# A hybrid decoder layer with 32 experts: blocks in the order of their numbers, earlier weight loads, five seams rearranged

## The chip, the cores and the metric

The kernel runs on one core of one Trainium2 chip. The metric is the device time of one execution in microseconds. Before the change three runs took 1807.75 to 1808.81 us, with a median of 1807.97 us. The engines are TensorE (PE), VectorE (DVE), ScalarE (ACT), GpSimd (POOL) and SyncE (SP, which here only issues DMAs).

## The reference

One layer on x of 1024 tokens by 1024 features, in float32:

```
h = rms_norm(x, g);  proj = h @ w_in          # q, k, v of four mixers, and 4 x 1024 gate columns
o_swa = sliding-window attention (128 back, sinks, T5 bias)
o_fox = forgetting attention;  o_sb = stick-breaking attention
o_dsa = attention on the 256 best keys of an indexer, T5 bias
merged = sum over the 4 branches b of sigmoid(gate_b) * (o_b @ w_branch[b])
x = x + merged @ w_out
h2 = rms_norm(x, g2)
# 32 experts in 4 groups: best group, its 2 best experts, weights from both softmaxes
# assignments sorted by expert, each expert's padded to blocks of 128 tokens; block i, of expert e:
  g, u = split(h2[tokens of i] @ w_up[e], 2);  y = (silu(g) * u) @ w_down[e]
x = x + weighted sum of each token's two y
```

An expert's `w_up` is 1024 x 1024 and its `w_down` 512 x 1024, 6 MB in all.

## The kernel before

**Products.** Operands are kept as two parts that TensorE takes, a high one that ScalarE writes by rounding and a low one that VectorE or GpSimd writes as the difference. Each product is three matmuls: high by high, and high by low both ways.

**Stages.** `build` runs stages one after the other. Between two of them all engines meet at a barrier.

- `project` norms and turns the eight x tiles (SyncE's first issues, then `turn_x` on TensorE), makes V tile by tile, then 17 pieces of q and k columns and the indexer's scores. ScalarE's high parts and GpSimd's low parts of the weight pieces run ahead of TensorE.
- `select_and_gate` multiplies 32 pieces of gate columns, each 48 matmuls of 128x512 (`sg_gp`, lines 83 to 85), ScalarE takes the sigmoid and the tile is stored. Behind piece 0 TensorE makes the small T5 products of line 893, for which two tables are loaded. VectorE picks the best 256 keys all through this stage.
- `mix` does the attention head by head, then merges the branches: for each of 8 column blocks k and 4 branches j, 12 matmuls into `at_sps` (two banks by turns), which VectorE multiplies by a gate tile in `selm` and adds up (lines 1506, 1511, 1515). VectorE also makes the low part of the next branch weights (`wb_lo`, line 1463, after j = 2) and at some blocks that of an output weight (`wo_lo`, after j = 1). The output projection, the norm and the router follow tile by tile; SyncE stores x2 and h2 of each tile.
- `route_and_experts` counts the experts' tokens, places them (VectorE, a list of small steps), and runs the blocks.

**The experts.** Each block needs four pairs of up weights and two of down weights, 1 MB each. They pass through `WeightRing`: 12 raw places that SyncE loads (`load_pair`, line 1762), then 4 places with the parts (`split_high`, line 1766, ScalarE; `split_low`, line 1770, VectorE). SyncE waits for the low part of what lay in a place before. An expert's number comes from a plan (`eblk`). Before the plan is made, SyncE can load only expert 0's pairs, in the routing stage. All blocks of an expert follow one another, and experts are taken in the order 0, 8, 16, 24, 1, 9, ... (`spread`, `stride`).

GpSimd gathers the tokens of blocks 0 and 1 (line 2139) by numbers that VectorE finds (`find_next`, `number_tokens`) with sums by TensorE (`sum_ids`), and writes 16 notes, one for each tile of tokens and choice, into `slots` (line 2144). Later blocks read their token ids from `slots`, so these must have landed. Two empty scatters to the output open the row of scatters (line 2134), which go one after another since a token can be in two blocks. The loop then runs two blocks a trip. A block is `turn_x`, `up` (48 matmuls into `ex_gp`, `ex_upp`), `turn_a`, and `down` (24 matmuls into `ex_yp`); ScalarE's `silu` and `scale` (line 2247) stand between. The block after has its `up` ahead of this block's `down`. The last two blocks are written out behind the loop.

## Time and profile before

| what | value |
| --- | --- |
| median of 3 runs | 1807.97 us |
| the profiled execution's own time | 1811.79 us |
| its span in the profile | 1810.1 us |
| TensorE busy | 1695.0 us, 94% |
| VectorE, ScalarE, GpSimd busy | 1268.5 (70%), 859.0 (47%), 348.6 (19%) |
| DMA | 361.72 MB, mean 200 GB/s |
| ScalarE's high part of an expert pair (L1766), mean of 192 | 1915 ns |
| VectorE's low part of one (L1770), mean of 192 | 2288 ns |
| landing of an up pair, a down pair, median | 20.7, 21.2 us |
| mean granted clock of TensorE | 0.976 |

The page cuts the span in 40 slices of 45 us. In most of them TensorE is busy nine tenths or more:

```profile
PE   6999998999999988899998999677999999999995
DVE  4023678799999508877657753486898989888883
GB/s 198 90 109 170 79 136 116 133 118 93 93 94 93 130 91 170 82 106 140 144 13 228 225 128 125 202 326 317 383 370 374 352 362 346 363 346 365 366 361 55
```

The projection takes slices 1 to 7, the gates 8 to 15, attention 16 to 21, merging, output projection and router 22 to 25, the routing 26 and 27, and the experts the rest. A digit is the busy share of a slice in tenths, 9 for 90% or more. Busy time of an engine that nobody waits for costs nothing, so what counts is who waits for whom at a given moment; the timeline gives that, with the idle time ahead of an instruction and what released it in brackets.

### The profile page before, as it was taken

Reading aid. Unit: us, or ns where it says so; the run is one execution under the profiler, and the core shown is the slowest. Engines: PE = TensorE matmul, PEld = TensorE weight load, DVE = VectorE, ACT = ScalarE, POOL = GpSimd, SP = SyncE. Lnnn points to the kernel's source line nnn. Section 1 sums busy time; section 2 is a strip of 40 time slices with the busy share of each in tenths; the row PEclk is TensorE's granted clock in tenths of the full one; section 3 lists DMA queues with packets and bytes.
Section 4 is the critical chain, followed back from the end, with each engine's and each line's share of the span. In section 5 each row is a group of like instructions: output and inputs, shape, how many; then the busy total and the mean of one; then the engine's idle time right before and its main releaser. Section 6 shows DMA issues by size and latency. Waiting matters only on the chain. (4 is left out here: it accounts for less than half of the span.)

```text
span 1810.1 us, 25235 instructions
## 1 busy us (share of the span) xinstructions
PE 1695.0 (94%) x8628; PEld 1405.5 (78%) x8628; DVE 1268.5 (70%) x1693; ACT 859.0 (47%) x1034; POOL 348.6 (19%) x289
## 2 busy tenths in 40 slices
PE   6999998999999988899998999677999999999995
PEld 5887777787888877799986778566888888877784
DVE  4023678799999508877657753486898989888883
ACT  6114552211112215567851112345888887777773
POOL 3111122232222210100010000173222222222221
PEclk9999999999999998999999999878999999999997
DMA  5236233332222437346506634588999999999992
GB/s 198 90 109 170 79 136 116 133 118 93 93 94 93 130 91 170 82 106 140 144 13 228 225 128 125 202 326 317 383 370 374 352 362 346 363 346 365 366 361 55
DMA packets 110578, 361.72 MB, mean 200 GB/s; under 512 B 18731, under 2 KB 22827, under 8 KB 110496
## 3 DMA queue, kind: packets, MB, share of 16 engines
q1 hardware_dynamic: 97508, 342.52, 54.4%
q0 software_dynamic: 12992, 18.14, 4.2%
q8 instruction: 51, 0.84, 0.2%
q14 instruction: 27, 0.22, 0.0%
HBM read 315.51 MB, written 63.96 MB: 210 GB/s over the span
## 5 line engine op out<-in xcount | busy, mean ns | idle before, releaser
L1770 DVE TENSOR_TENSOR ex_wl<-ex_raw,ex_wh 128x2048 fp32r<-128x2048 f32 x192 | 436.5, 2288 | 92.1 <-ACT ex_wh L1766 89.1
L1766 ACT ACTIVATE ex_wh<-ex_raw 128x2048 fp32r<-128x2048 f32 x192 | 367.3, 1915 | 110.6 <-DMA ex_raw<-in_w_expert_up 53.3
L83 PE MATMUL sg_gp<-hT_hi,gs_wh 128*128 128x512 f32 x512 | 200.8, 392 | 6.7 <-PEq L66 6.7
L84 PE MATMUL sg_gp<-hT_lo,gs_wh 128*128 128x512 f32 x512 | 200.2, 391 | 0.0
L85 PE MATMUL sg_gp<-hT_hi,gs_wl 128*128 128x512 f32 x512 | 200.0, 391 | 0.0
L793 ACT ACTIVATE gs_wh<-gs_raw 128x1024 fp32r<-128x1024 f32 x30 | 31.8, 1061 | 263.9 <-PE sg_gp L85 263.9
L857 DVE MATCH_REPLACE8 selm<-sg_top,selm 128x512 f32<-128x512 f32 (+5 forms) x160 | 138.6, 872 | 0.0
L853 DVE MAX8 sg_top<-selm 128x8 f32<-128x512 f32 (+5 forms) x160 | 133.9, 876 | 0.0
L2335 PE MATMUL ex_gp<-ex_wh,ex_xh 128*128 128x512 f32 x256 | 109.0, 426 | 17.6 <-DVE ex_wl L1770 14.6
L1627 PE MATMUL at_ops<-at_v,at_pT 128*128 128x65 f32 (+1 forms) x984 | 125.0, 269 | 0.0
L1627 PEld LDWEIGHTS at_ops<-at_v,at_pT 128*128 128x128 f32 x984 | 120.5, 192 | 0.7
L737 POOL TENSOR_TENSOR gs_wl<-gs_raw,gs_wh 128x1024 fp32r<-128x1024 f32 x30 | 72.2, 2405 | 251.2 <-ACT gs_wh L793 251.2
L83 PEld LDWEIGHTS sg_gp<-hT_hi,gs_wh 128*128 128x128 f32 x512 | 96.7, 189 | 28.1 <-issue 8.0
L84 PEld LDWEIGHTS sg_gp<-hT_lo,gs_wh 128*128 128x128 f32 x512 | 96.7, 189 | 20.4 <-issue 0.2
L85 PEld LDWEIGHTS sg_gp<-hT_hi,gs_wl 128*128 128x128 f32 x512 | 96.7, 189 | 20.2
L590 PE MATMUL pj_ps<-hT_hi,gs_wh 128*128 128x512 f32 x272 | 110.5, 406 | 0.0
L2335 PE MATMUL ex_yp<-ex_wh,ex_ah 128*128 128x512 f32 x256 | 102.2, 399 | 7.8 <-DVE ex_al L2046 7.8
L591 PE MATMUL pj_ps<-hT_lo,gs_wh 128*128 128x512 f32 x272 | 106.1, 390 | 0.0
L592 PE MATMUL pj_ps<-hT_hi,gs_wl 128*128 128x512 f32 x272 | 106.1, 390 | 0.0
L2134 POOL DMA_INDIRECT out_x<-ex_xa,ex_ids_o x32 | 57.4, 1794 | 235.7 <-ACT ex_xa L2247 235.4
L2335 PE MATMUL ex_upp<-ex_wh,ex_xh 128*128 128x512 f32 x256 | 102.0, 398 | 0.0
L2337 PE MATMUL ex_gp<-ex_wh,ex_xl 128*128 128x512 f32 x256 | 101.8, 398 | 0.0
(311 smaller groups left out, 3672.3 us busy)
## 6 DMA issues: line engine op xcount, KB each, us to landing
ex_raw<-in_w_expert_up SPq DMA_DIRECT2D x128, 1024.0 KB, 20.7
ex_raw<-in_w_expert_down SPq DMA_DIRECT2D x64, 1024.0 KB, 21.2
gs_raw<-in_w_gate SPq DMA_DIRECT2D x32, 512.0 KB, 3.5
gatesT<-sg_go SPq DMA_DIRECT2D x32, 512.0 KB, 2.6
selm<-gatesT SPq DMA_DIRECT2D x32, 512.0 KB, 5.9
at_qk<-qkh SPq DMA_DIRECT2D x52, 256.0 KB
at_qk<-qkl SPq DMA_DIRECT2D x44, 256.0 KB
gs_raw<-in_w_qk SPq DMA_DIRECT2D x17, 512.0 KB, 4.9
```

Source lines behind the costliest of these rows:

```text
L83: pe.matmul(out, a_hi, b_hi, start=(k == 0), stop=False)
L84: pe.matmul(out, a_hi, b_lo, start=False, stop=False)
L85: last = pe.matmul(out, a_lo, b_hi, start=False, stop=(k == len(lhs) - 1))
L590: pe.matmul(out, wh[k % 2][:, q, :], hT[0][:, q, cols], start=(q == 0), stop=False)
L591: pe.matmul(out, wh[k % 2][:, q, :], hT[1][:, q, cols], start=False, stop=False)
L592: last = pe.matmul(out, wl[k % 2][:, q, :], hT[0][:, q, cols], start=False, stop=(q == KC - 1))
L853: dve.max(top8[j][:, :], acc).then_inc(picked, 1)
L857: dve.match_replace(acc, top8[j][:, :], acc, PICKED).then_inc(picked, 1)
L1627: last = pe.matmul(o_ps[u % 2][:, 0:width], pT[u % 2][:, j, :], values[:, kb, f:f + width], start=(j == 0), stop=(j == len(ks) - 1))
L1766: act.activation(ring.wh[r][:, :, :], ring.raw[slot][:, :, :], ACT.Copy).then_inc(ring.w_high, 1)
L1770: dve.tensor_tensor(ring.wl[r][:, :, :], ring.raw[slot][:, :, :], ring.wh[r][:, :, :].bitcast(F32), ALU.subtract).then_inc(ring.w_low, 1)
L2335: pe.matmul(bank, hi[:, k, :], wh[r][:, i, cols], start=(k == 0), stop=False)
```

## The change

1. **Start.** The gain vector is issued second and x tile 1 fourth; TensorE turns two tiles before the first V tile, not three.
2. **Projection to gates.** The banks of both stages are the same now, and `project` multiplies gate piece 0 at its end.
3. **Gates to attention.** GpSimd writes the two one-column memsets of `keep` before the four large ones.
4. **Merging.** `wb_lo` goes after j = 1 and `wo_lo` after j = 2.
5. **Early loads.** The ring's raw places have a fixed address from the start, in an order in which four of them are free in `mix`: expert 0's up pairs are loaded behind tiles 1 to 4 of h2.
6. **Order of the experts.** Block e, for e under 32, is the first block of expert e; further blocks of an expert follow from block 32 on. So expert 1's up pairs are loaded without the plan. VectorE has four steps more, two on 128x256 numbers and two on small ones.
7. **Routing.** `sum_ids(2)` comes after the first up pair, ScalarE makes three high parts before the last exponential, and TensorE runs 11 matmuls whose result nobody uses (`keep_busy`) around the first `turn_x`.
8. **End.** The last block's down weights are split earlier, its turned activations go to block x's buffers (`xh`, `xl`), its matmuls go to `ex_gp` and `ex_upp`, and `turn_a` of the last block stands between the two down pairs of the one before. The last scaling is done in two halves.

The diff, cut to its core:

```diff
@@ -275,9 +277,9 @@
                     sp.dma_start(o[k], t[:, :].bitcast(F32)).then_inc(stored, 16)
             load_x(0)
+            sp.dma_start(g[:, :], a["norm_mix_g"].to_broadcast([P, D])).then_inc(g_loaded, 16)
+            load(0)
             load_x(1)
-            load(0)
-            sp.dma_start(g[:, :], a["norm_mix_g"].to_broadcast([P, D])).then_inc(g_loaded, 16)
             load_x(2)
...
-            for t in range(3):
-                turn_x(t)
-            turns = [{1: 3, 5: 4}, {1: 5, 5: 6}, {1: 7}]
+            turn_x(0)
+            turn_x(1)
+            turns = [{1: 2, 5: 3}, {1: 4, 5: 5}, {1: 6, 5: 7}]
...
+            pe.wait_ge(w_low, GATE_PIECE + 1)
+            pe.wait_ge(rectified, len(UNITS))
+            side = GATE_PIECE % 2
+            for h in range(2):
+                cols = slice(h * HALF, (h + 1) * HALF)
+                multiply(pe, si[:, cols], [(wh[side][:, q, :], wl[side][:, q, :]) for q in range(KC)],
+                         [(hT[0][:, q, cols], hT[1][:, q, cols]) for q in range(KC)])
...
+            pe.sem_inc(gated, 2)
             for k in range(NG):
                 pe.wait_ge(w_low, GATE_PIECE + k + 1)
                 for h in range(2):
+                    if k == 0:
+                        continue
...
+                if 1 <= tile <= len(IN_ROUTE):
+                    load_pair(sp, a, ring, IN_ROUTE[tile - 1], 0, tile - 1)
...
+            for s in range(2):
+                pool.memset(keep[s][:, T:T + 1], 1.0).then_inc(made, 1)
+            pool.wait_ge(made, 2)
             slots.zero(pool, (2, 3))
             pool.wait_ge(slots.zeroed, 8)
-            for s in range(2):
-                pool.memset(keep[s][:, T:T + 1], 1.0).then_inc(made, 1)
...
-                if j == 2 and 2 <= k + 1 < KC:
+                if j == 1 and 2 <= k + 1 < KC:
                     wb_lo(k + 1)
-                if j == 1 and k in (2, 4, 6):
+                if j == 2 and k in (2, 4, 6):
                     wo_lo(k // 2)
...
@@ -1884,22 +1911,19 @@
         position = lambda b, j: (b + 1) * PAIRS + j
         place = lambda s, j: ((s + 1) % 2 * PAIRS + j) % RAW
         SKIPPED = UP_PAIRS
-        CONSTS = 14
+        CONSTS = 16
         marks = {}
         @block.sync
         def _(sp):
-            for j in IN_ROUTE:
-                load_pair(sp, a, ring, j, 0, j - FIRST)
             for j in range(UP_PAIRS, PAIRS):
                 load_pair(sp, a, ring, PAIRS + j, 0, j)
+            for j in range(UP_PAIRS):
+                load_pair(sp, a, ring, place(0, j), 1, j)
             sp.wait_ge(planned, 1)
             sp.wait_ge(gathered[0], 16)
             n = trips(sp)
             expert = lambda b: sp.value_load(eblk[0:1, bass.ds(b, 1)], min_val=0, max_val=EXPERTS - 1)
-            e = expert(1)
-            for j in range(UP_PAIRS):
-                load_pair(sp, a, ring, place(0, j), e, j)
...
+            step(dve.scalar_tensor_tensor(base[:, :], base[:, :], float(P), to_end[:, :], ALU.mult, ALU.add))
             dve.wait_ge(ranked, 1)
-            step(dve.scalar_tensor_tensor(slot, base[:, :].unsqueeze(1).to_broadcast([P, NT, EXPERTS]), float(P), ranks,
-                                          ALU.mult, ALU.add))
+            E = [P, NT, EXPERTS]
+            step(dve.scalar_tensor_tensor(slot, ranks, P - 0.5, base[:, :].unsqueeze(1).to_broadcast(E), ALU.is_ge, ALU.mult))
+            step(dve.tensor_tensor(slot, slot, ranks, ALU.add))
+            step(dve.tensor_tensor(slot, slot, first[:, :].unsqueeze(1).to_broadcast(E), ALU.add))
...
+            step(dve.tensor_tensor(ebcol[:, :], ebcol[:, :], own[:, :], ALU.add))
...
+            find_next(3)
             x_lo(1, 1)
-            find_next(3)
-            number_tokens(3)
             low(0, 0, 0)
             gate_up(0, position(0, 0))
+            number_tokens(3)
...
+            low(n * 2 + 1, 1, UP_PAIRS, SKIPPED)
             gate_up(n * 2 + 1, position(n * 2, UP_PAIRS))
-            for j in range(UP_PAIRS, PAIRS):
-                low(n * 2 + 1, 1, j, SKIPPED)
-            a_lo(n * 2 + 1)
+            low(n * 2 + 1, 1, UP_PAIRS + 1, SKIPPED)
+            a_lo(n * 2 + 1, xh[0], xl[0])
...
-            const(pool.memset(steps[:, 0:1], -1.0))
-            const(pool.memset(stride[:, :].rearrange("p (j q) -> p j q", q=GROUPS)[:, 0:PER_GROUP - 1, GROUPS - 1],
-                              1.0 - PER_GROUP * (GROUPS - 1)))
+            const(pool.memset(steps[:, 0:1], 4.0 * T))
+            const(pool.affine_select(out=own[:, :], in_=own[:, :], compare_op=ALU.is_ge, fill=0.0, base=EXPERTS - 1,
+                                     pattern=[[0, 1]], channel_multiplier=-1))
+            const(pool.iota(first[:, :], pattern=[[P, EXPERTS]], base=0, channel_multiplier=0, **F))
+            const(pool.iota(to_end[:, :], pattern=[[-P, EXPERTS]], base=(EXPERTS - 1) * P, channel_multiplier=0, **F))
...
-            const(pool.iota(bcol[:, :], pattern=[[0, 1]], base=0, channel_multiplier=1, **F))
-            const(pool.iota(evens[:, :], pattern=[[2, MAX_BLOCKS // 2]], base=0, channel_multiplier=0, **F))
+            const(pool.iota(bcol[:, :], pattern=[[0, 1]], base=-EXPERTS, channel_multiplier=1, **F))
+            const(pool.iota(evens[:, :], pattern=[[2, MAX_BLOCKS // 2]], base=-EXPERTS, channel_multiplier=0, **F))
...
-            high_in_route(IN_ROUTE[0])
+            for p in IN_ROUTE[:3]:
+                high_in_route(p)
             act.wait_ge(d, marks["ratio"])
             act.activation(rinv[:, :, :], ratio[:, :, :], ACT.Exp).then_inc(e_done, 1)
-            for p in IN_ROUTE[1:]:
-                high_in_route(p)
+            high_in_route(IN_ROUTE[3])
...
+            def last_high(j):
+                act.wait_ge(w_loaded[place(1, j)], loads(n, 1))
+                act.wait_ge(used, position(n * 2, j - 1))
+                split_high(act, ring, place(1, j), place(1, j) % RING)
+            last_high(UP_PAIRS)
             silu(n * 2 + 1)
+            last_high(UP_PAIRS + 1)
+            a_hi(n * 2 + 1, xh[0])
             scale(n * 2, 0, n, position(n * 2, PAIRS))
-            for j in range(UP_PAIRS, PAIRS):
-                act.wait_ge(w_loaded[place(1, j)], loads(n, 1))
-                act.wait_ge(used, position(n * 2, j))
-                split_high(act, ring, place(1, j), place(1, j) % RING)
-            a_hi(n * 2 + 1)
-            scale(n * 2 + 1, 1, n, position(n * 2 + 1, PAIRS) - SKIPPED)
+            act.wait_ge(ids_o_loaded[1], n * 16 + 16)
+            act.wait_ge(scattered[1], n * 16 + 16)
+            for h, bank in enumerate((gp, upp)):
+                act.wait_ge(last_made, h + 1)
+                last = act.activation(xa[1][:, h * HALF:(h + 1) * HALF], bank[:, :], ACT.Copy,
+                                      scale=ids_o[1][:, 1:2].bitcast(F32))
+            last.then_inc(scaled, 1)
...
+                if j == 0:
+                    sum_ids(2)
                 if j == 1:
                     turn_x(1, 1, 16)
-                    sum_ids(2)
+            def keep_busy(n):
+                for _ in range(n):
+                    pe.matmul(gp[:, :], ones[:, :], full[:, :, :, :].rearrange("p k t e -> p (k t e)"), start=True, stop=True)
...
+            keep_busy(6)
             turn_x(0, 0, 16)
+            keep_busy(5)
             up(0, 0, FIRST, FIRST, between)
...
-            down(n * 2, 0)
-            turn_a(n * 2 + 1)
-            down(n * 2 + 1, 1, SKIPPED)
+            down(n * 2, 0, lambda j: turn_a(n * 2 + 1) if j == UP_PAIRS else None)
+            pe.wait_ge(a_low, n * 2 + 2)
+            pe.wait_ge(w_low, position(n * 2 + 1, UP_PAIRS) + 1 - SKIPPED)
+            for h, bank in enumerate((gp[:, :], upp[:, :])):
+                cols = slice(h * HALF, (h + 1) * HALF)
+                for k in range(FC):
+                    if (h, k) == (0, PAIR):
+                        pe.wait_ge(w_low, position(n * 2 + 1, UP_PAIRS + 1) + 1 - SKIPPED)
+                    r = place(1, UP_PAIRS + k // PAIR) % RING
+                    pe.matmul(bank, xh[0][:, k, :], wh[r][:, k % PAIR, cols], start=(k == 0), stop=False)
+                    pe.matmul(bank, xh[0][:, k, :], wl[r][:, k % PAIR, cols], start=False, stop=False)
+                    last = pe.matmul(bank, xl[0][:, k, :], wh[r][:, k % PAIR, cols], start=False, stop=(k == FC - 1))
+                last.then_inc(last_made, 1)
```

VectorE's list in the merging of branches, from block k = 2 to k = 3, before (`mg_sum` and `at_v`/`at_o` are gated products and sums, `mg_wb_low` and `or_wo_low` the two low parts):

```order
L1506 TENSOR_TENSOR mg_sum<-at_sps,selm 128x1024
L1511 TENSOR_TENSOR at_v<-at_sps,selm 128x1024
L1515 TENSOR_TENSOR mg_sum<-mg_sum,at_v 128x1024
L1463 TENSOR_TENSOR or_wo_low<-or_wo_raw,or_wo_high 128x1024
L1511 TENSOR_TENSOR at_o<-at_sps,selm 128x1024
L1515 TENSOR_TENSOR mg_sum<-mg_sum,at_o 128x1024
L1463 TENSOR_TENSOR mg_wb_low<-mg_wb_raw,mg_wb_high 128x1024
L1511 TENSOR_TENSOR at_v<-at_sps,selm 128x1024
L1515 TENSOR_TENSOR mg_sum<-mg_sum,at_v 128x1024
```

The same place of the change:

```order
L1522 TENSOR_TENSOR mg_sum<-at_sps,selm 128x1024
L1527 TENSOR_TENSOR at_v<-at_sps,selm 128x1024
L1531 TENSOR_TENSOR mg_sum<-mg_sum,at_v 128x1024
L1479 TENSOR_TENSOR mg_wb_low<-mg_wb_raw,mg_wb_high 128x1024
L1527 TENSOR_TENSOR at_o<-at_sps,selm 128x1024
L1531 TENSOR_TENSOR mg_sum<-mg_sum,at_o 128x1024
L1479 TENSOR_TENSOR or_wo_low<-or_wo_raw,or_wo_high 128x1024
L1527 TENSOR_TENSOR at_v<-at_sps,selm 128x1024
L1531 TENSOR_TENSOR mg_sum<-mg_sum,at_v 128x1024
```

The branch weights' low part now stands two operations earlier, ahead of the third branch.

ScalarE's list behind the loop, before (`ex_gl` is the SiLU, `ex_xa` the scaled result, `ex_ah` the high part of the turned activations):

```order
L2235 ACTIVATE ex_gl<-ex_gp 128x512
L2246 REGISTER_ALU
L2247 ACTIVATE ex_xa<-ex_yp,ex_ids_o 128x1024
L2277 REGISTER_ALU
L2278 REGISTER_ALU
L1766 ACTIVATE ex_wh<-ex_raw 128x2048
L2278 REGISTER_ALU
L1766 ACTIVATE ex_wh<-ex_raw 128x2048
L2239 ACTIVATE ex_ah<-ex_ap 128x512
L2246 ISA
L2247 ACTIVATE ex_xa<-ex_yp,ex_ids_o 128x1024
```

The same place of the change:

```order
L1789 ACTIVATE ex_wh<-ex_raw_53 128x2048
L2265 REGISTER_ALU
L2266 ACTIVATE ex_gl<-ex_gp 128x512
L2307 REGISTER_ALU
L1789 ACTIVATE ex_wh<-ex_raw_54 128x2048
L2270 ACTIVATE ex_xh<-ex_ap 128x512
L2277 REGISTER_ALU
L2278 ACTIVATE ex_xa<-ex_yp,ex_ids_o 128x1024
L2319 ACTIVATE ex_xa<-ex_gp,ex_ids_o 128x512
L2319 ACTIVATE ex_xa<-ex_upp,ex_ids_o 128x512
```

Both high parts now stand ahead of the scaling of the block before, the first one ahead of the SiLU.

## Rows read from the trace of the kernel before

**Rows 1.** Expert loop: stretch, length, busy PE PEld DVE ACT POOL, PEclk, DMA share, GB/s.

```profile
1260.00:1440.00 180.00, 180.00 (x854) 149.04 (x853) 159.99 (x92) 145.25 (x101) 40.33 (x40) 1.00 1.01 371
1470.00:1700.00 230.00, 225.08 (x1051) 183.53 (x1051) 195.03 (x111) 176.36 (x124) 55.80 (x51) 1.00 0.99 358
```

**Rows 2.** Timeline, start: start, duration, engine, line, operation, [idle before, its releaser].

```profile
9.16 4.01 DVE L447 SCALAR_TENSOR_TENSOR pj_x<-pj_x,pj_rs,pj_g 128x1024 f32<-128x1024 f32 x2 [9.16 <-DMA pj_g<-in_norm_mix_g]
...
24.38 2.55 POOL L336 TENSOR_TENSOR pj_vl<-gs_raw,pj_vh 128x1024 fp32r<-128x1024 f32 x1 [0.83 <-ACT pj_vh L362]
```

**Rows 3.** Timeline, border from projection to gates, TensorE and VectorE.

```profile
318.27 0.77 PE L83 MATMUL sg_gp<-hT_hi,gs_wh 128*128 128x512 f32 x1 [6.68 <-PEq L66]
...
323.76 1.21 DVE L816 TENSOR_TENSOR sg_fg<-sg_fhl 4x1024 f32<-4x1024 f32 x1 [4.23 <-DMA sg_fbias<-in_forget_bias]
...
331.70 1.45 PE L893 MATMUL sg_tp<-sg_onehot,sg_table 33*4 33x384 f32 x4
```

**Rows 4.** Busy time by stretches, within the gates' stage.

```profile
450.00:600.00 150.00, 150.00 (x663) 124.20 (x662) 149.97 (x275) 28.35 (x42) 32.08 (x14) 1.00 0.27 95
```

**Rows 5.** Timeline, border from gates to attention.

```profile
682.74 0.42 DVE L1417 TENSOR_TENSOR_SCAN at_keep<-at_t 128x128 f32<-128x128 f32 x1 [68.12 <-POOL at_keep L1281]
...
683.54 0.48 PE L1602 MATMUL at_tps<-ident,at_x 128*128 128x128 f32 x1 [2.00 <-DVE at_x L1421]
```

**Rows 6.** TensorE's waits from 960 to 1045: total us, count, longest.

```profile
PE at_sps L83 <- DVE mg_wb_low L1463: 8.1, 6, 1.8
```

**Rows 7.** Timeline, merging: first and last of six waits, a gate tile.

```profile
967.28 0.50 PE L83 MATMUL at_sps<-o_hi,mg_wb_high 128*128 128x512 f32 x1 [0.97 <-DVE mg_wb_low L1463]
...
978.77 0.33 SPq L1208 DMA_DIRECT2D mg_wb_raw<-in_w_br  x1
...
983.63 1.22 DVE L1506 TENSOR_TENSOR mg_sum<-at_sps,selm 128x1024 f32<-128x1024 f32 x1 [0.86 <-DMA selm<-gatesT]
...
1031.70 0.50 PE L83 MATMUL at_sps<-o_hi,mg_wb_high 128*128 128x512 f32 x1 [1.70 <-DVE mg_wb_low L1463]
```

**Rows 8.** Waits of SyncE's queue, 1150 to 1250: total us, count, longest.

```profile
SPq L1762 <- DVE ex_wl L1770: 41.5, 12, 16.9
```

**Rows 9.** Timeline, routing and the first blocks of the experts.

```profile
1168.89 0.42 DVE L1980 SCALAR_TENSOR_TENSOR ex_xa<-rt_base,ex_yp 128x256 f32<-128x256 f32 x1
...
1195.38 1.05 POOL L2139 DMA_INDIRECT ex_xg<-h2d,rt_found  x1 [5.09 <-DVE rt_found L1995]
...
1238.98 1.11 ACT L2247 ACTIVATE ex_xa<-ex_yp,ex_ids_o 128x1024 f32<-128x1024 f32 x1 [14.62 <-DMA out_x<-ex_xa,ex_ids_o]
...
1244.27 0.80 PE L2335 MATMUL ex_gp<-ex_wh,ex_xh 128*128 128x512 f32 x1 [9.55 <-DVE ex_wl L1770]
```

**Rows 10.** Chain that ended last, 1155 to 1262: start, us, what.

```profile
1222.33 7.81 DMA slots<-rt_entry,rt_pos
...
1231.89 6.92 DMA out_x<-ex_xa,ex_ids_o
```

**Rows 11.** Timeline, TensorE behind a short idle, between the first two blocks.

```profile
1203.46 0.77 PE L2362 MATMUL ex_ap<-ident,ex_act 128*128 128x128 f32 x4 [3.19 <-DVE ex_act L2042]
...
1205.36 0.63 PE L2336 MATMUL ex_gp<-ex_wl,ex_xh 128*128 128x512 f32 x1
```

**Rows 12.** Timeline, the end.

```profile
1783.22 4.49 DVE L1770 TENSOR_TENSOR ex_wl<-ex_raw,ex_wh 128x2048 fp32r<-128x2048 f32 x2 [6.36 <-ACT ex_wh L1766]
...
1788.45 0.79 PE L2335 MATMUL ex_yp<-ex_wh,ex_ah 128*128 128x512 f32 x1 [7.77 <-DVE ex_al L2046]
...
1798.99 1.59 POOL L2134 DMA_INDIRECT out_x<-ex_xa,ex_ids_o  x1 [15.10 <-ACT ex_xa L2247]
```

**Rows 13.** One tile's issues and landings: last two down pairs, then the last scatter.

```profile
L1762 SPq DMA_DIRECT2D ex_raw<-in_w_expert_down x2: 1851/1937/2023, 1756.4 to 1758.6; - x2
...
DMA to landing us min/median/max: 19.0/19.7/20.5
...
DMA to landing us min/median/max: 6.4/6.4/6.4
```

More of the change, by code:

```diff
@@ L144, in __init__ @@
         self.out_parts = [sb(f"gs_out{part}", [P, T], FR) for part in ("_hi", "_lo")]
+        self.banks = [c.enter_context(nc.psum_tensor(f"gs_banks{s}", [P, KC, P], F32)) for s in range(2)]
         self.w_loaded = [sem(f"gs_w_loaded{s}") for s in range(3)]
@@ L2350, in up, with down @@
                         between(j)
-            def down(b, s, skipped=0):
+            def down(b, s, between=None):
                 pe.wait_ge(a_low, b + 1)
```

66 lines of the change are left out of this document (40 added, 26 removed).

## The prediction

> **What bounds the kernel now.** I read the page first: TensorE is busy 94% of the span. Such a share says little alone, so the next view is the busy time by stretches. Between 1260 and 1440 us TensorE is never idle while the DMA engines are full (share 1.01); from 1470 to 1700 they are still full and TensorE idles 4.9 us [rows 1]. So the experts run on two resources that are nearly equal, and giving one of them room can't bring much there. Most of the 115 us of TensorE idle lie elsewhere, in waits at the borders of stages. I then read the timeline at each border that the diff touches. The reader should see in each who releases TensorE, and who is next in line just behind: that decides how much of a wait is to be had. A result within 0.2% (3.6 us) is what a measurement of this kernel can't tell from no change.
>
> **Start.** VectorE waits until 9.16 for the gain vector, issued behind two x tiles and a weight piece [rows 2]. The change issues it second, and TensorE begins the first V tile after two turned tiles instead of three. But TensorE's way through that tile ends with GpSimd's low part of weight piece 3, at 24.38 + 2.55 = 26.93 [rows 2]. That part follows ScalarE's serial list (roots and high parts), full from 14 us on. In the new issue order x tile 1 comes last of the four, so I take this list as about 2 us earlier and piece 3 as 1.7 earlier. The tile turned later costs its eight transposes then, 0.7. **Gain 1.0**; ends 0 (x tile 1 as late as the gain vector is now, ScalarE unmoved) and 2.5.
>
> **From projection to gates.** TensorE idles 6.68 before 318.27 [rows 3]. The change puts gate piece 0 (48 matmuls at 150 / 663 = 0.226 [rows 4], 10.9 us) ahead of the barrier. The hole is shorter than the work: TensorE ends at 311.6 + 10.9 = 322.5, and with 1.3 for the barrier the next stage starts at 323.8, 5.5 later than now. There a wait comes out that was hidden. The small matmuls (331.70, 1.45) need the one-hot and T5 tables, which SyncE issues in the new stage behind the forget bias; VectorE got that bias at 323.76, 5.5 after the stage began [rows 3]. Until now 13 us of gate matmuls covered this. Now TensorE stands to about 323.8 + 6.1 = 329.9, and starts at half clock: small matmuls to 332.3, piece 1 10.9, plus 1.1 for its matmuls at half clock, so 344.3 against 331.70 + 1.4 + 10.9 = 344.0. **Loss 0.3**: a stall moved, not removed. Ends: loss 2, gain 1.5 (tables 2 us sooner). By the Trainium skill, DMA: Bandwidth & Descriptors, "Anatomy of one DMA", a transfer has a fixed cost of about 2 us; by that rule the tables are there some 4 us into the stage, and the part gains about 1.7. The 5.5 us of the row speak against it.
>
> **From gates to attention.** VectorE's first scan waits for two tiny memsets of GpSimd, which stand behind four large ones: it starts at 682.74, and TensorE, idle 2.00, at 683.54 [rows 5]. Put first, they are done before the first sigmoid is. What is late next is V, loaded in this stage: TensorE's first product with it would come 2 us sooner, and V maybe 1. The large memsets end 0.4 later; the loads behind them serve head 2, some 40 us on. **Gain 1.5**; ends 0.9 and 2.0.
>
> **Merging the branches.** Six times TensorE waits at a block's first product for the low part of the next branch weights, 8.1 us in all [rows 6]. The five blocks from 967.28 to 1031.70 take 12.88 each [rows 7]; their 48 matmuls take 10.9. The change makes that low part one branch earlier and the output weight's one later, as the order excerpt shows, and this wait ends. Late next is the gate tile: SyncE issues it only when the previous block's products are done (issues begin 978.77), and VectorE starts on it at 983.63, 4.9 later [rows 7]. The gated product ends 1.22 after, 6.1 after the block's start; TensorE's third product reuses that bank and could start at 5.5. So 0.6 or more of each wait comes back, and 0.3 in blocks where VectorE also carries the output weight (nine operations of about 1.2: 10.7 of 10.9). 12.88 becomes 11.8 to 11.9: five blocks give 5.0, the first 0.4. **Gain 5.4**; ends 3 and 8.1.
>
> **Routing, and the start of the experts.** Four early loads of 1 MB and expert 1's first four fill the ring sooner. Does this lead help later? SyncE waits 41.5 us for freed places before 1250, 16.9 of it at once [rows 8]: the ring of 12 is full already when the loop gets going. **So the early loads are worth nothing by themselves**; the lead that counts is the ring's size. What holds the loop is another chain: GpSimd's gather at 1195.38, then twelve notes and a gather, the last note landing 7.81 after 1222.33, the ids, two empty scatters landing 6.92 after issue; ScalarE scales at 1238.98 and TensorE, idle 9.55, starts at 1244.27 [rows 9, 10]. Three things move it. The added VectorE steps (two like the one at 1168.89, of 0.42 and a gap, two of some 0.2) delay it by 1.35. The gather of block 2 needs its token numbers, which the new order sums after one pair instead of two, with TensorE at full clock; GpSimd idles 5.09 there [rows 9]. VectorE's list after its routing steps (three low parts of 2.2, the low part of x, a search of 2.7, one more low part) ends at 1193.2, so the gather starts at 1194.2, 1.1 earlier. Last, with the weights ahead, 4 MB less are queued while notes and ids land. With nothing queued the last scatter landed in 6.4 [rows 13]; I take 2.3 off the three landings together. **Gain 3.4**; ends: loss 1 (only the added steps), gain 6.5 (every landing as with nothing queued).
>
> **End.** Now the last block's down weights are split only after the block before is scaled: VectorE's two low parts start at 1783.22, behind ScalarE's two; TensorE idles 7.77 before its last 24 matmuls, and the last scatter starts at 1798.99 [rows 12]. The new end splits these weights earlier and sums into free banks. But their loads are issued at 1756.4 and 1758.6 and land 19.0 and 20.5 later, 1775.4 and 1779.1 [rows 13]. ScalarE's list has the first split ahead of the SiLU: split (1.9, the mean of its 192) to 1777.4, SiLU 1778.0; VectorE's low part (2.2) to 1779.7, the product 1780.4. TensorE is done with the first down pair at 1777.4 (down ends at 1780.1 now, a pair is 2.7) and stands 3 us for the transposes. After 3.19 us of idle it ran at half clock (0.63 a row, starts 0.43 apart) [rows 11], so I take that again: second pair to 1786.1, block 30's scatter, some 2 us after, at 1788.2. It must land (6.5) before the last one starts: about 1795.0. The last products are done near 1791.8 and scaled by 1793.3; they no longer end last. **Gain 4.0**; ends 2, and 7.6 (clock kept: 1784.7 + 6.5).
>
> **Sum.** 1.0 - 0.3 + 1.5 + 5.4 + 3.4 + 4.0 = 15.0 us. The profiled execution took 1811.8; it becomes 1796.8. The median of the three runs lies 3.8 below that execution, so I forecast **1793 us**.
>
> **Rivals.** (A) The lead does count: 4.2 MB at 371 GB/s [rows 1] are 11 us of DMA work done early, and the 6 us that TensorE idles for weights late in the loop vanish: 15.0 + 6 gives 1787. For it: the DMA engines are the late bound. Against it: rows 8. Chance 0.10. (B) Covers hold everywhere: merging 8.1 and the end 7.6 give 6.3 more, 1787; with the tables early 1785. Against it: the second waiter in rows 7 and 13. Chance 0.15. (C) Covers fail: start 0, gates -2, merging 3, routing 0.5, the end 2, attention 1.5, so a gain of 5 and 1803. For it: each seam has a second waiter within 1 to 2 us. Chance 0.16. (D) Slower: in the order of numbers experts read neighbouring weights, where now the order strides over eight. If that costs DMA rate, it does so from 1244 to 1764, at 358 to 371 GB/s now [rows 1]. To lose the 15.0 in 520 us the mean rate must fall by 3%, under about 350; at 4% it is 20.8 longer, 1814. No row shows it; against it, each load is 1 MB in either order. Chance 0.03. (E) The change reorders the program but frees no wait that ends last: within 3.6 us, 1808. Chance 0.03.
>
> **Numbers.** The forecast, 1789 to 1797, has 0.53. The range 1784 to 1800 takes in A, most of B and the near part of C, and leaves out the rest. Faster by over 0.2%: 0.53 + 0.10 + 0.15 + 0.16 = 0.94; no change 0.03; slower 0.03.
>
> **What would show it.** Right: TensorE idle some 6 us inside the gates' stage before the small matmuls; no wait for the branch weights' low part, but short ones for a gated bank; the ring full before the loop, with ScalarE's first scale some 3 us earlier in the routing; TensorE idle about 3 us between the last two down pairs, and the last scatter waiting for the one before. Wrong: no idle at the small matmuls; no TensorE idle late in the loop (A); a DMA rate under 350 GB/s there (D); merging blocks still at 12.9 us, or at 10.9 (B).

## The result, and the profile after

Seven runs of the changed kernel took 1792.7 to 1805.9 us, with a median of 1801.6; seven of the kernel before 1807.4 to 1811.4, median 1808.5. The ratio is 0.9944, with a 95% interval of 0.9928 to 0.9960: 10.1 us faster, or 7 to 13. The two medians by themselves lie 6.9 apart, at the lower end of that interval. The forecast was 15, with 8 to 24 as its range. In these runs the changed kernel scatters over 13 us where the one before scatters over 4; the traces of the experiments point at a cause.

The page of the changed kernel, with the profiled execution at 1804.9 us:

```profile
span 1803.3 us, 25241 instructions
...
PE 1706.3 (95%) x8639; PEld 1405.0 (78%) x8639; DVE 1269.5 (70%) x1697; ACT 860.2 (48%) x1035; POOL 350.7 (19%) x292
...
PE   7999999899999998899999999688999999999995
...
PEclk9999999899999998999999999889999999999998
...
GB/s 194 97 112 171 80 130 117 134 118 93 94 94 93 124 98 170 83 106 132 153 13 210 246 152 176 190 298 299 376 369 372 358 363 352 351 356 353 366 354 76
```

TensorE is busy 11 us **longer** than before, at the same number of real products. That is the first thing to notice: something made its work slower. To find where the time went I took the same event in both traces at each border, and subtracted. Both profiled executions lie 3.3 us above the medians of their kernels, so the gains add up to 6.8, and each is read from one pair of traces.

| event (first of its kind) | before | after | gained so far | in this part | forecast |
| --- | --- | --- | --- | --- | --- |
| q and k products | 91.76 | 90.19 | 1.6 | 1.6 | 1.0 |
| attention, first scores | 679.07 | 677.75 | 1.3 | -0.3 | -0.3 |
| merging, first product | 941.49 | 939.95 | 1.5 | 0.2 | 1.5 |
| output projection | 1045.12 | 1042.84 | 2.3 | 0.7 | 5.4 |
| routing, first count | 1166.27 | 1165.48 | 0.8 | -1.5 | 0 |
| first up product | 1184.69 | 1185.20 | -0.5 | -1.3 | |
| turn_x of block 4 | 1260.40 | 1254.15 | 6.2 | 6.8 | 3.4 with the line above |
| turn_x of block 31 | 1751.28 | 1746.51 | 4.8 | -1.5 | 0 |
| end of the span | 1810.1 | 1803.3 | 6.8 | 2.0 | 4.0 |

The rows of the timeline of the changed kernel that answer to [rows 3], [rows 5] and [rows 7]:

```profile
326.88 2.71 PE L905 MATMUL sg_tp<-sg_onehot,sg_table 33*4 33x384 f32 x4 [5.99 <-DMA sg_table<-in_t_table]
...
679.24 0.42 DVE L1433 TENSOR_TENSOR_SCAN at_keep<-at_t 128x128 f32<-128x128 f32 x1 [65.95 <-ACT at_t L1310]
...
682.97 0.69 PE L1643 MATMUL at_ops<-at_v,at_pT 128*128 128x64 f32 x2 [0.96 <-DMA at_v<-vtok]
...
972.83 0.80 PE L83 MATMUL at_sps<-o_hi,mg_wb_high 128*128 128x512 f32 x1 [2.26 <-DVE mg_sum L1522]
...
1044.75 0.63 PE L1686 MATMUL at_tps<-or_wo_low,at_qk 128*128 128x512 f32 x1
```

And of its waits from 940 to 1043 (engine, line, waited for: total us, times, longest), VectorE's longest, which answers to [rows 6]:

```profile
DVE mg_sum L1522 <- DMA selm<-gatesT: 13.5, 6, 4.0
```

Each forecast stall is there, under its new name: 5.99 for the T5 tables, V's landing behind the first scans, a gated bank in the merging. The timeline's last row was not foreseen: a product of 0.63 us, 2 us behind the start of the output projection. In the kernel before, the same 1.96 us wait stands ahead of the output projection and no product slows down.

The loop, three products of block 6 in the changed kernel, then in the kernel before:

```profile
1310.75 0.40 PE L2382 MATMUL ex_gp<-ex_wh,ex_xh 128*128 128x512 f32 x1
1310.99 0.39 PE L2383 MATMUL ex_gp<-ex_wl,ex_xh 128*128 128x512 f32 x1
1311.22 0.40 PE L2384 MATMUL ex_gp<-ex_wh,ex_xl 128*128 128x512 f32 x1
1311.45 0.39 PE L2382 MATMUL ex_upp<-ex_wh,ex_xh 128*128 128x512 f32 x1
```

```profile
1311.09 0.39 PE L2335 MATMUL ex_gp<-ex_wh,ex_xh 128*128 128x512 f32 x1
1311.33 0.39 PE L2336 MATMUL ex_gp<-ex_wl,ex_xh 128*128 128x512 f32 x1
1311.55 0.39 PE L2337 MATMUL ex_gp<-ex_wh,ex_xl 128*128 128x512 f32 x1
1311.78 0.39 PE L2335 MATMUL ex_upp<-ex_wh,ex_xh 128*128 128x512 f32 x1
```

The starts stand 0.70 apart over three products after, 0.69 before. Over the whole loop the mean is 0.2333 against 0.2290 us a product, and the block takes 18.11 us against 17.81, to the hundredth, block after block. Nothing in the diff touches the loop's instructions.

### The profile page after: what moved, and what is told of

It reads as the page before. It is cut to its first block and busy times, and to the rows that moved or that the text cites. A ratio compares the mean times of both kernels' runs of the same rounds, so it can differ in the third digit from the quotient of the medians.

```text
span 1803.3 us, 25241 instructions
## 1 busy us (share of the span) xinstructions
PE 1706.3 (95%) x8639; PEld 1405.0 (78%) x8639; DVE 1269.5 (70%) x1697; ACT 860.2 (48%) x1035; POOL 350.7 (19%) x292
## 5 line engine op out<-in xcount | busy, mean ns | idle before, releaser
L1789 ACT ACTIVATE ex_wh<-ex_raw 128x2048 fp32r<-128x2048 f32 x192 | 367.2, 1915 | 99.7 <-PE ex_upp L2384 37.0
L83 PE MATMUL gs_banks<-hT_hi,gs_wh 128*128 128x512 f32 x512 | 200.7, 392 | 0.0
L84 PE MATMUL gs_banks<-hT_lo,gs_wh 128*128 128x512 f32 x512 | 200.1, 391 | 0.0
L85 PE MATMUL gs_banks<-hT_hi,gs_wl 128*128 128x512 f32 x512 | 199.9, 390 | 0.0
L83 PEld LDWEIGHTS gs_banks<-hT_hi,gs_wh 128*128 128x128 f32 x512 | 96.6, 189 | 21.8 <-issue 1.5
L84 PEld LDWEIGHTS gs_banks<-hT_lo,gs_wh 128*128 128x128 f32 x512 | 96.7, 189 | 20.3 <-issue 0.2
L85 PEld LDWEIGHTS gs_banks<-hT_hi,gs_wl 128*128 128x128 f32 x512 | 96.7, 189 | 20.1
L2383 PE MATMUL ex_upp<-ex_wl,ex_xh 128*128 128x512 f32 x256 | 102.0, 399 | 0.0
```

The lines of the kernel that those rows point to most:

```text
L83: pe.matmul(out, a_hi, b_hi, start=(k == 0), stop=False)
L84: pe.matmul(out, a_hi, b_lo, start=False, stop=False)
L85: last = pe.matmul(out, a_lo, b_hi, start=False, stop=(k == len(lhs) - 1))
L1789: act.activation(ring.wh[r][:, :, :], ring.raw[slot][:, :, :], ACT.Copy).then_inc(ring.w_high, 1)
L2383: pe.matmul(bank, hi[:, k, :], wl[r][:, i, cols], start=False, stop=False)
```

## The experiments

x64, split, t5later, gatefirst, gateonly, endswap, nobusy and keepback were executed once each: 1799.5, 1805.6, 1794.3, 1794.4, 1799.5, 1797.1, 1799.1 and 1803.2 us. All lie in the range of the changed kernel's own seven runs, so they are read by the stretch that their edit touches, and not by their whole time. Where a stretch of the program is the same in several kernels, their traces also show how much it varies by itself.

**What slows the products, and what it costs.** The change takes the experts' weight places to another address, and all that is allocated behind them moves. The stationary operands xh, xl, ah and al start 64 bytes past a multiple of 128 in the kernel before, and 96 past one in the changed kernel.

x0, the changed kernel with 32 bytes more (x64 is the same with 96 bytes, `[P, 24]`):

```diff
+        sb("ex_pad", [P, 8])
         xh = [sb(f"ex_xh{s}", [P, KC, P], FR) for s in range(2)]
```

> The changed kernel with 32 unused bytes ahead of the experts' activations, so that xh, xl, ah and al (the stationary operands of the 72 products of a block) start at a multiple of 128 bytes; in the kernel before they start 64 past one, in the changed kernel 96 past one. Theory P (the place of the stationary operand sets the pace): the products follow each other in 0.227 us, as in the gates' stage where the stationary operands are at such places, against 0.229 before and 0.233 in the changed kernel; a block of the first half of the loop takes 17.6 to 17.8 us, not 18.1. Theory Q (the pace comes from something else of the change: the experts read in another order, loads running ahead): 0.233 and 18.1 as in the changed kernel. For the whole time P says little: if DMA sets the end of the loop, the last blocks slow to 18.9 earlier and the kernel gains 0 to 3 us on the changed one; if TensorE sets it, 8 to 11.

> The same with 96 unused bytes, so that these operands start 64 bytes past a multiple of 128, as in the kernel before. Theory P: 0.229 us between products and 17.8 us a block. Theory Q: 0.233 and 18.1.

b96 is the kernel before with the same line.

> The kernel before with 32 unused bytes, so that these operands start 96 bytes past a multiple of 128, as in the changed kernel; nothing else of the change. Theory P: 0.233 us between products, 18.1 us a block in the first half of the loop; the whole slower by 0 to 3 us if DMA sets the loop's end. Theory Q: 0.229 and 17.8, the time of before.

split has that line, and ahead of `ah` another, `sb("ex_pad2", [P, 24])`.

> The changed kernel with xh and xl at a multiple of 128 bytes (32 unused bytes ahead of them) and ah and al 96 past one (96 more bytes ahead of them). Theory P, of the stationary operand alone: up products 0.227 us apart, down products 0.233. If instead the pace hangs on the whole layout (VectorE, ScalarE and DMA writing elsewhere), both kinds of product keep one pace.

| kernel | up products | down products | a block, first half | slows from block | turn_x of 4 to 31 | ratio to before |
| --- | --- | --- | --- | --- | --- | --- |
| before | 0.229 | 0.229 | 17.81 | 22 | 490.9 | |
| b96 | 0.233 | 0.233 | 18.11 | 27 | 490.4 | 1.0002 [0.9992, 1.0013] |
| changed | 0.233 | 0.233 | 18.11 | 26 | 492.4 | 0.9944 [0.9928, 0.9960] |
| x64 | 0.233 | 0.233 | 18.12 | 26 | 492.0 | |
| split | 0.228 | 0.234 | 17.87 | 22 | 491.7 | |
| x0 | 0.228 | 0.227 | 17.70 | 19 | 493.0 | 0.9936 [0.9920, 0.9952] |

```profile
1296.55 1.04 PE L2325 MATMUL ex_xp<-ident,ex_xg 128*128 128x128 f32 x8
...
1314.66 1.03 PE L2325 MATMUL ex_xp<-ident,ex_xg 128*128 128x128 f32 x8
...
1332.76 1.04 PE L2325 MATMUL ex_xp<-ident,ex_xg 128*128 128x128 f32 x8
```

These are `turn_x` of three blocks in b96: 18.11 apart, where only 32 unused bytes differ from the kernel before. Theory Q falls: the order of the experts has no part in it. That it is the stationary operand is shown by split, in which up and down products of one block have two paces. Where exactly the good places lie is open: x64 should have given 0.229 by my rule and gave 0.233, so the distance to a multiple of 128 is not the rule. A multiple of 128 was the best of the places tried (here it is one of 256 as well). The Trainium skill, SBUF — State Buffer, section "Operand start alignment", asks only for a multiple of the element size, and says that this is about legality, not speed; the runs agree with the first, and for the speed they show 0.227 to 0.234 us between legal places.

The other half of the table matters more. **The pace is worth nothing here.** b96 is slower than the kernel before in each block up to 21 and takes the same time; x0 is faster than the changed kernel in each up to 18, and its time can't be told from the changed kernel's. All six need 490 to 493 us for the 27 blocks. A kernel with quick products uses up the lead of its ring sooner, and then goes at 19 us a block, at the pace of the loads. So the loop's length is set by DMA, as its end in [rows 1] said; what TensorE does in between decides only when that shows. How near the two are is seen in noearly (below): its loop starts 4.2 us later, only one of its blocks goes over 18.11 us (18.59), and 27 blocks take 489.4, which is TensorE's pace. TensorE's 11 us more on the page are mostly these products (30 blocks at 0.30 make 9, the dummy products of the routing 4), and they cost nothing.

**The T5 tables.** t5later:

```diff
-                if k == 0:
+                if k == 1:
                     pe.wait_ge(small_loaded, 32)
```

> The changed kernel with the small T5 products behind gate piece 1 instead of piece 0. My theory of this seam: the change moved gate piece 0 ahead of the barrier, and TensorE then had nothing to cover the landing of the T5 tables, so that of 6.7 us idle 6.0 came back. Then piece 1 starts 1.3 us behind the last product of the projection, the tables are there when piece 1 ends, and the attention starts 4 to 6 us sooner than in the changed kernel (at about 672 to 674 us, not 677.8). Rival: what holds is the low part of piece 2, which GpSimd makes in this stage behind its load; then TensorE stands there instead, and the attention starts at 676 or later.

```profile
322.21 0.47 PE L83 MATMUL gs_banks<-hT_hi,gs_wh 128*128 128x512 f32 x1 [1.24 <-PEq L66]
...
333.28 1.45 PE L905 MATMUL sg_tp<-sg_onehot,sg_table 33*4 33x384 f32 x4
...
335.95 0.50 PE L83 MATMUL gs_banks<-hT_hi,gs_wh 128*128 128x512 f32 x1 [1.22 <-POOL gs_wl L746]
```

Gate piece 1 follows the barrier after 1.24 us, and the tables are there when it ends. The rival's wait exists and is 1.22 long. The attention starts at 671.04, 6.7 us sooner than in the changed kernel (4 to 6 were expected): with the 5.99 of idle, 11 products at half clock (329.5 to 334.0 in the changed kernel) went too. The span was 1792.7.

**The merging of branches.** gatefirst, SyncE's list:

```diff
-                if j == 0 and k + 1 < KC:
-                    sp.wait_ge(multiplied, n)
-                    load_wb(k + 1)
                 sp.wait_ge(gated, n - 3)
                 load_gate(n)
+                if j == 1 and k + 1 < KC:
+                    sp.wait_ge(multiplied, n - 1)
+                    load_wb(k + 1)
```

> The changed kernel with SyncE issuing a block's first two gate tiles ahead of the wait for the block before, and the next branch weights behind them. My theory of the merging: the gate tile took the place of the weights' low part as the last thing waited for, since SyncE issues it only when the block before is done. Then TensorE's waits for mg_sum (4 us in the changed kernel) go, a block takes 11.2 to 11.5 us (48 products of 0.233), and from the first product of the merging to the output projection it takes 96 to 99 us, not 102.9. Rival 1: VectorE's nine operations a block hold it (10.7 us): same. Rival 2: the branch weights now come late: TensorE waits for their low part again, 102 us or more.

gateonly is gatefirst with `wb_lo` and `wo_lo` where they stood before the change.

> As gatefirst, but with the low parts on VectorE in the order of before (wb_lo after j = 2, wo_lo after j = 1): part 4 of the change undone, the gate tiles early. From the first product of the merging to the output projection the kernel before takes 103.6 us, the changed kernel 102.9, gatefirst 93.8. Theory: the two are in series, and each needs the other: without the swap TensorE still waits 1.0 and 1.7 us by turns for the low part (8.1 us in all), so 101 to 103 us. Rival: the low part came late only because VectorE itself started a block late, behind the gate tile; then the swap is worth little, and it takes 94 to 97 us.

| gate tiles | low part after j = 2 (before) | low part after j = 1 (the change) |
| --- | --- | --- |
| behind the branch weights | before: 103.6 us | changed: 102.9 us |
| ahead of them | gateonly: 102.6 us | gatefirst: 93.8 us |

TensorE's waits from 940 to the end of the merging, in gateonly and in the changed kernel (in gatefirst there is none but 0.6 us at the start):

```profile
PE at_sps L83 <- DVE mg_wb_low L1479: 8.0, 6, 1.7
```

```profile
PE at_sps L83 <- DVE mg_sum L1522: 5.6, 6, 2.3
```

Two waits stood one behind the other. Taking either alone gave 0.7 and 1.0 us in these traces; both gave 9.8. The eight other kernels that merge exactly as the changed kernel does take 99.7 to 105.6 us, with 3.7 to 8.1 us of waits for a gated bank, so the change's part 4 alone is worth -2 to 4 us, 1.7 in the mean. gatefirst's 93.8 lies clear of them all, best (below) has 93.9, and gatefirst is better than its theory had it (96 to 99). The place to look was [rows 7]: a gate tile is issued only once the branch weights ahead of it in SyncE's list may be issued.

**The end.** endswap:

```diff
-            last_high(UP_PAIRS)
             silu(n * 2 + 1)
+            last_high(UP_PAIRS)
...
-            low(n * 2 + 1, 1, UP_PAIRS, SKIPPED)
             gate_up(n * 2 + 1, position(n * 2, UP_PAIRS))
+            low(n * 2 + 1, 1, UP_PAIRS, SKIPPED)
```

> The changed kernel with the last block's SiLU and gated product ahead of the split of its first down pair, on ScalarE and VectorE. My theory: the 4.5 us that TensorE stands ahead of the last turn_a, and the half clock behind them, come from that split, whose load lands late. Then TensorE has no wait there above 1 us, the scatter of block 30 starts 8 to 8.5 us after the first product of its second down pair would now (measured from turn_x of block 31, at 33 to 34 us, not 38.5), and the span ends 4 to 6 us sooner than it would. Rival: the landing of the last loads holds the last block anyway, and the end comes 1 to 2 us sooner.

The timeline of the changed kernel, then of endswap:

```profile
1773.06 1.91 ACT L1789 ACTIVATE ex_wh<-ex_raw 128x2048 fp32r<-128x2048 f32 x1 [2.73 <-DMA ex_raw<-in_w_expert_down]
...
1777.96 0.93 PE L2411 MATMUL ex_ap<-ident,ex_act 128*128 128x128 f32 x4 [4.51 <-DVE ex_act L2070]
...
1785.04 1.60 POOL L2165 DMA_INDIRECT out_x<-ex_xa,ex_ids_o  x1 [10.32 <-ACT ex_xa L2278]
...
1792.40 1.59 POOL L2165 DMA_INDIRECT out_x<-ex_xa,ex_ids_o  x1 [5.77 <-issue]
```

```profile
1776.44 1.60 POOL L2165 DMA_INDIRECT out_x<-ex_xa,ex_ids_o  x1 [4.36 <-ACT ex_xa L2278]
...
1784.49 1.59 POOL L2165 DMA_INDIRECT out_x<-ex_xa,ex_ids_o  x1 [6.46 <-ACT ex_xa L2319]
```

In the changed kernel the SiLU stands behind a split whose load lands at 1773.06, and the last scatter behind the landing of the one before. In endswap block 30's scatter starts 32.0 us behind `turn_x` of block 31 (38.5 in the changed kernel), and the last one no longer waits for it but for its own scaling. From that `turn_x` to the end of the span it takes 51.0 us, against 56.8 in the changed kernel and 58.8 before.

Most of these 5.8 us can't be put down to the edit. Ten traces have the end exactly as the changed kernel has it. They take 52.2 to 56.8 us there, 54.1 in the mean, and TensorE's wait ahead of the last `turn_a` is 1.9 to 4.6 us: the changed kernel's own trace is one of the two longest. In five of the ten the clock falls once more there (54.4 to 56.8), in five it doesn't (52.2 to 53.2). The two traces with the swap take 51.0 (endswap, no fall) and 54.5 (best, with one). So the swap moves the scatter of block 30 (32.0 and 33.3, against 34.5 to 39.3), but for the end it is worth 1 to 2 us as far as twelve traces tell, which is what the rival expected, and the theory's 4 to 6 isn't shown.

**The early loads.** noearly:

```diff
-                if 1 <= tile <= len(IN_ROUTE):
-                    load_pair(sp, a, ring, IN_ROUTE[tile - 1], 0, tile - 1)
...
+            for j in IN_ROUTE:
+                load_pair(sp, a, ring, j, 0, j - FIRST)
             for j in range(UP_PAIRS, PAIRS):
```

> The changed kernel without the four early loads behind the tiles of h2: expert 0's up pairs are loaded in the routing stage, as before; all else stays. My theory of the prediction (the ring is full before the loop in either case, so the early loads alone are worth nothing at the end of the loop): the same time as the changed kernel within 2 us; the first up products 0 to 2 us later. Rival A (the lead counts, 4 MB): up to 11 us slower. Rival on the landings: with 4 MB more queued in the routing, notes and ids land later, and the loop starts 2 to 4 us later than in the changed kernel (turn_x of block 4 at 1256 to 1258, not 1254).

The ratio to the kernel before is 0.9963 [0.9951, 0.9974], 3.4 us above the changed kernel's, with intervals that overlap; the first up products come 2.9 us later behind the start of the routing. From the start of the routing to block 4 the kernel before takes 94.1 us, the changed one 88.7, noearly 93.2; but from there to block 31 noearly needs 489.4, three less. So the loads are worth 4.5 us at the start of the loop, near what the rival on the landings expected (2 to 4), and 1.5 of that is left at its end. My theory is half confirmed: within 2 us by the trace at the loop's end, not shown by the ratio (3.4), and the first up products come later than its 0 to 2. Rival A's 11 us fall. Two steps of the chain of waits, in the changed kernel and in noearly (start, us, what), answer to [rows 10]:

```profile
1222.08 5.98 DMA slots<-rt_entry,rt_pos
...
1229.82 2.12 DMA out_x<-ex_xa,ex_ids_o
```

```profile
1225.20 6.43 DMA slots<-rt_entry,rt_pos
...
1233.39 2.14 DMA out_x<-ex_xa,ex_ids_o
```

The scatter lands in 2.1 us in both, against 6.9 before. So the early loads did not do this. What is left is expert 1's first pairs, which no longer wait for the plan: the ring is full sooner, and the DMA engines run dry while TensorE works. No run undoes that part alone, so this cause is argued and not shown. The busy time from 1230 to 1240, before and after (length, busy time of the engines, clock, DMA share, GB/s):

```profile
1230.00:1240.00 10.00, 4.72 (x25) 3.64 (x23) 0.00 (x0) 1.02 (x2) 4.88 (x6) 0.90 0.85 331
```

```profile
1230.00:1240.00 10.00, 3.68 (x11) 2.67 (x10) 4.93 (x3) 7.88 (x7) 8.64 (x7) 0.77 0.27 57
```

The early loads do another thing: without them the last note starts 3.1 us later (1225.20).

**Work that keeps TensorE busy.** nobusy:

```diff
-            keep_busy(6)
             turn_x(0, 0, 16)
-            keep_busy(5)
```

> The changed kernel without the 11 matmuls that keep TensorE busy around the first turn_x (keep_busy). They run about 3 us of TensorE time in a wait. If they hold the clock, the first up products fall to half clock without them, as in the kernel before (12 products of 0.43 us, 2.4 us lost by the clock), and turn_x of block 1 comes 1.5 to 2.5 us later against the start of the routing than in the changed kernel (29.2 us). If the loop start is held by notes and landings, turn_x of block 4 keeps its distance from the start of the routing (88.6 to 89 us) all the same.

```profile
1183.67 0.80 PE L2382 MATMUL ex_gp<-ex_wh,ex_xh 128*128 128x512 f32 x1 [2.44 <-DVE ex_xl L2065]
1184.26 0.63 PE L2383 MATMUL ex_gp<-ex_wl,ex_xh 128*128 128x512 f32 x1
```

The clock does fall without them, for 12 products, as before the change. With them it falls too, only later (7 products from 1191.3). `turn_x` of block 1 comes 28.4 us behind the start of the routing, 0.7 **sooner** than in the changed kernel, so this prediction failed; block 4 comes at 89.0 against 88.7, which is the second theory. In x0, split and gatefirst, which have the dummy products too, the clock doesn't fall at 1191 and block 1 comes at 27.6; their block 4 comes at 88.2, 88.4 and 91.0. So the dummy products hold the clock in some executions, and at block 4 they buy less than 1 us.

**The memsets.** keepback:

```diff
+            slots.zero(pool, (2, 3))
+            pool.wait_ge(slots.zeroed, 8)
             for s in range(2):
                 pool.memset(keep[s][:, T:T + 1], 1.0).then_inc(made, 1)
-            pool.wait_ge(made, 2)
-            slots.zero(pool, (2, 3))
-            pool.wait_ge(slots.zeroed, 8)
```

> The changed kernel with the two one-column memsets behind the four large ones again, as before. The changed kernel gained 2.2 us up to the first scan and lost it again behind the first product with V. My theory: V's landing and TensorE's clock set this seam, so from the start of the attention to the first product of the merging it takes the same 262.2 to 262.4 us. Rival (the prediction's): the memsets are worth 1.5 us, and it takes 263.7 or more.

Measured: 267.2 us, which the rival would claim; but the trace says otherwise. The same transposes of the first head come 37.95 us behind the start of the attention in the changed kernel and 38.05 in keepback: the memsets are worth 0.1. The rest comes later, at 740 to 760, here in the changed kernel and in keepback:

```profile
740.00:760.00 20.00, 17.51 (x137) 15.05 (x137) 17.07 (x25) 10.60 (x20) 0.00 (x0) 1.00 0.40 84
```

```profile
740.00:760.00 20.00, 19.71 (x109) 17.71 (x109) 12.46 (x20) 7.33 (x15) 0.00 (x0) 0.66 0.27 52
```

The granted clock is 0.66 of full over this stretch, TensorE does 109 products instead of 137, and 5 us are gone. split shows the same 5 us at the same place (267.6), best a shorter stretch of this kind (263.7); the other eleven traces don't (260.8 to 262.4). Both have the same waits of 1.0 to 1.4 us ahead of this stretch; in the one the clock fell behind them, in the other it did not.

**All together.** best has the line of x0, t5later, gatefirst and endswap.

> The changed kernel with four edits together: 32 unused bytes ahead of the experts' activations, the T5 products behind gate piece 1, the first two gate tiles of a block issued ahead of the branch weights, the last block's SiLU and gated product ahead of its first split. Alone, they brought the attention 6.7 us forward, the output projection 8.7, the end 5.9, and the pace of products from 0.233 to 0.227 without a gain. My theory: the seams ahead of the loop add up to 13 to 15 us, since the loop takes 490 to 493 us from turn_x of block 4 to that of block 31 whatever its pace (DMA sets its end), and the end adds 5: 1780 to 1786 us, a ratio of 0.983 to 0.987 to the kernel before. Rival: the notes and ids of the routing take their time whatever comes before, or the loads do, so that half of the 14 us is lost at the start of the loop: 1788 to 1792, 0.988 to 0.991.

It took 1785.7 us (1784.1 to 1790.8), ratio 0.9864 [0.9841, 0.9887]: 24.6 us faster than the kernel before, and the fastest of all. Up to the routing it is 14.5 us ahead of the changed kernel, at `turn_x` of block 31 16.0, at the end 18.3. So nothing of the lead was lost on the way, and the rival's loss of half of it did not come; only the upper end of the ratio's interval (0.9887) touches the rival's range. The parts, of one trace each, say the same less sharply: t5later had 5.6 us at the routing and 6.2 at block 31, gatefirst 8.7 and 6.0.

## Why the prediction was right, and where it was not

**The direction and the range of the gain held**, 10.1 us inside 8 to 24, and what each seam would wait for next was named at all five. They held narrowly: the median of 1801.6 us lies 1.6 above the range of 1784 to 1800, and it is the ratio, taken of the 1808.0 that the forecast started from, that gives 1797.8. Some luck is in it, since the routing and the start of the loop gave 5.5 for 3.4, for a reason that was not foreseen, and made up for part of the merging and the attention. The sum came out half too high: these two terms were too large, and the fall of the clock at the output projection was not in it.

- **Start**, 1.0 forecast: 1.6 measured (0.9 to 1.6 in twelve traces). ScalarE's list came 2.4 us sooner, not 1.7.
- **Projection to gates**, -0.3: -0.3. "A stall moved, not removed": 5.99 of idle at the tables, the small products at half clock. Table and stage were 5.1 us apart (issue of the stage's first load at 321.80, small products at 326.88), between the row's 5.5 and my estimate of 4, for which I had leaned on the fixed cost of about 2 us in the Trainium skill, DMA: Bandwidth & Descriptors, "Anatomy of one DMA". That section gives its figure for transfers that GpSimd issues. SyncE issues these tables, the second at 323.6, and the products start 3.3 us behind that.
- **Gates to attention**, 1.5: 0.2. The scans did start sooner (679.24, 1.5 us behind TensorE's first scores, 3.7 before). The step that failed is "V maybe 1": behind V's 0.96 TensorE stayed at half clock until 689.7, where the kernel before was at full clock from 688.5. In gateonly the clock was back at 681.7, and there the attention took 260.8 us, 1.6 less than before: about the 1.5 of the forecast.
- **Merging**, 5.4: 0.7 in this trace, 1.7 in the mean of nine. This is the largest error. "Late next is the gate tile" was right, but it was priced as if it were ready 4.9 us after its issue in each block. The load took 6.3 (the page's median), SyncE's issue slid with the block that it waits for, and one stall of 2.26 cost seven more products at half clock. A wait that feeds back on its own cause can't be priced from one instance.
- **Output projection**, not in the sum: -1.5. Eight products at half clock from 1044.3. It isn't tied to an edit: five of the twelve traces have it (122.6 us from the start of the output projection to the routing), the other seven take 121.0 to 121.1, as before.
- **Routing and the start of the loop**, 3.4: 5.5 together. The added steps cost 1.3, as forecast (1.35). The gather came 1.3 sooner (27.8 us behind the start of the routing, 29.1 before; 1.1 forecast), but GpSimd then waited again ahead of the next one, and the last note left 0.5 later than before. The landings gave 6.6 (7.81 + 6.92 against 5.98 + 2.12), not 2.3. The row I leaned on, 6.4 for the last scatter with nothing queued, was that of a full scatter; an empty one landed in 2.1 with the DMA engines nearly idle (share 0.27), and that they would be so I had not seen.
- **Loop**, 0: -1.5, inside what six traces differ by (490.4 to 493.0).
- **End**, 4.0: 2.0 in this trace, 5 in the mean of ten (54.1 us against 58.8 and 59.5 in the two traces of the old end), so this term was sound. In this trace TensorE stood 4.5 us, not 3, and at half clock; the last scatter did wait for the one before, 7.4 us behind it and not 6.8.

Of the rivals, C (covers fail) came nearest. In this pair of traces the end gave its 2, merging less than its 3 and attention less than its 1.5, while start, gates and routing did better than it said. "The early loads are worth nothing by themselves" was wrong for the start of the loop (4.5 us), and for the time 1.5 to 3.4 us are open. D and the order of the experts left no mark.

## What to carry to other kernels

Where a wait is removed, look for the list in which the second waiter's load stands, and price both waits as one: here 0.7 and 1.0 us apart, 9.8 together. What is saved ahead of a stage that DMA bounds arrives at its end; faster products inside it were worth nothing here. Before a term of 1 to 5 us is read from one trace, compare the same stretch in traces whose code is the same there: here it varied by 6 us in the merging and by 4.7 at the end. And when buffers move, compare the spacing of unchanged products before blaming the change's logic.

## What the runs showed of the hardware that I had not expected

The place of a stationary operand in a partition changes the spacing of 128x512 products of four-byte parts by 3%: 0.227 us at the best of the places tried, 0.233 to 0.234 at the worst, all legal, with the granted clock at 1.00 throughout.

The clock falls to half (1.2 GHz) behind waits of 1 to 3 us in some executions and not in others. The kernel before and b96 show such stretches (three products or more) at the same seven places each, with none between 689 and 1159. Eleven of the twelve traces of the changed kernel and what was made from it have one or two in attention, merging or output projection, at 730 to 755, 967 to 1018, or 1034 to 1047, worth 1.4 to 5 us; gateonly has none there. That is much of the scatter of 13 us, as far as the granted clocks of the seven runs tell: 0.978 for the run of 1805.9, 0.979 to 0.980 for the five from 1799.0 to 1804.9, 0.983 for the one of 1792.7. The kernel before scatters more in longer sets too: seventeen of its runs, taken beside x0, spread from 1808.0 to 1816.5. Whether the shorter waits at the seams make the fall more frequent, and why, was not settled.
